# Second block's attention: where the pieces of the differential values' projection are computed, how that half's value products are cut, and when kept results are split

## The reference

```python
out_a: sc = qg . ka * scale;  p = softmax(sc);  o = p @ va           # 8 heads of 64, 2 key/value heads
# out_b, the differential half: 4 heads, each with two score maps and values of width 128
sc = jnp.einsum('bqhjd,blhjd->bhjql', q, kb).astype(jnp.float32) * scale
p = jax.nn.softmax(sc, axis=-1)
w = (p[:, :, 0] - lam * p[:, :, 1]).astype(vb.dtype)
o = jnp.einsum('bhql,blhe->bqhe', w, vb)
o = rms_norm(o, subln_g) * (1.0 - lam_init)
...
x = x + jnp.einsum('ble,ed->bld', jnp.concatenate([out_a, out_b], axis=-1), w_out[l])
```

## Time and profile before

| | us |
|---|---|
| median of 3 runs | 2335.97 (2335.66 to 2338.61) |
| the profiled execution | 2333.98 |
| its span in the trace | 2332.20 |
| PE busy | 2273.7 (97% of the span) |
| attention loop, from the scores of step 0 to those of step 31 | 1767.08 to 1905.10 |
| start of the output projection after it | 1920.22 |

### The profile page before, as it was taken

The page is one execution under the profiler, slowest core; times in us unless marked ns, Lnnn a source line. Parts: engine busy times, 40 slices in busy tenths (PEclk is TensorE's granted clock), DMA queues, the critical chain, the costliest instruction groups (busy, mean ns, idle before and its releaser), DMA issues.

```text
span 2332.2 us, 30970 instructions
## 1 busy us (share of the span) xinstructions
PE 2273.7 (97%) x11139; PEld 1841.0 (79%) x11139; DVE 1007.9 (43%) x1598; ACT 613.0 (26%) x1083; POOL 1459.9 (63%) x1452
## 2 busy tenths in 40 slices
PE   8999999999999999999999999999999889999999
PEld 7767887888888887678878888888977557888887
DVE  6975553532331049657535333211384453333200
ACT  4333324221110023343242211110244552111100
POOL 6644665876667756546648767667493236767663
PEclk9999999999999999999999999999999999999999
DMA  5321333322332233212334232232330102332232
GB/s 183 100 72 55 95 103 112 133 97 93 99 99 92 98 116 101 72 55 95 96 117 137 91 99 98 91 99 92 121 114 16 37 1 77 104 99 95 94 100 81
DMA packets 69861, 217.37 MB, mean 93 GB/s; under 512 B 8448, under 2 KB 10752, under 8 KB 69632
## 3 DMA queue, kind: packets, MB, share of 16 engines
q1 hardware_dynamic: 54016, 188.41, 25.2%
q10 hardware_dynamic: 15744, 27.52, 3.3%
HBM read 195.93 MB, written 10.49 MB: 89 GB/s over the span
## 4 chain that ended last, share of the span: by engine, by line
PE 90%; DVE 6%; ACT 2%; issue 1%; ACTq 0%; DMA 0%; POOL 0%; DVEq 0%; POOLq 0%
PE ps L1665 78%; PE ps L1985 2%; PE ps L2150 2%; DVE score L1449 1%; DVE small L1445 1%; PE ps L1931 1%; ACT pe L1013 1%; PE ps L1916 1%; PE ps L2210 1%; PE ps L2170 1%; PE ps L1944 1%; PE ps L2028 1%; PE ps L2212 1%; PE ps L2015 0%; PE ps L2079 0%
## 5 line engine op out<-in xcount | busy, mean ns | idle before, releaser
L536 POOL TENSOR_TENSOR w_lo<-w_raw,w_hi 128x512 fp32r<-128x512 f32 x700 | 951.4, 1359 | 58.4
L533 POOL TENSOR_SCALAR w_hi<-w_raw 128x512 fp32r<-128x512 f32 x700 | 487.0, 696 | 680.1 <-DMA w_raw<-wst 651.3
L1665 PE MATMUL ps<-h_hi,w_lo 128*128 128x512 f32 (+1 forms) x2056 | 803.8, 391 | 20.0 <-issue 4.9
L1665 PE MATMUL ps<-h_lo,w_hi 128*128 128x512 f32 (+1 forms) x2056 | 784.9, 382 | 0.0
L1665 PE MATMUL ps<-h_hi,w_hi 128*128 128x512 f32 (+1 forms) x2056 | 784.8, 382 | 0.0
L1665 PEld LDWEIGHTS ps<-h_hi,w_lo 128*128 128x128 f32 x2056 | 387.5, 188 | 121.0 <-issue 33.4
L1665 PEld LDWEIGHTS ps<-h_lo,w_hi 128*128 128x128 f32 x2056 | 387.9, 189 | 77.7 <-issue 6.2
L1665 PEld LDWEIGHTS ps<-h_hi,w_hi 128*128 128x128 f32 x2056 | 387.4, 188 | 75.4
L1665 PE MATMUL ps<-a_hi,w_lo 128*128 128x512 f32 (+1 forms) x572 | 213.7, 374 | 0.0
L1665 PE MATMUL ps<-a_hi,w_hi 128*128 128x512 f32 (+1 forms) x572 | 213.2, 373 | 0.0
L1665 PE MATMUL ps<-a_lo,w_hi 128*128 128x512 f32 (+1 forms) x572 | 213.2, 373 | 0.0
(11 more groups left out here) (301 smaller groups left out, 2570.5 us busy)
## 6 DMA issues: line engine op xcount, KB each, us to landing
w_raw<-wst SPq DMA_DIRECT2D x350, 512.0 KB, 3.5
rot<-raw ACTq DMA_DIRECT2D x70, 128.0 KB, 3.3
gates<-gt ACTq DMA_DIRECT2D x32, 256.0 KB, 4.2
stage<-gates ACTq DMA_DIRECT2D x32, 256.0 KB, 3.0
x_sb<-xin SPq DMA_DIRECT2D x8, 256.0 KB, 5.6
out<-x_sb SPq DMA_DIRECT2D x8, 256.0 KB, 4.5
kc<-cst ACTq DMA_DIRECT2D x1, 1056.0 KB, 4.9
kc<-cst SPq DMA_DIRECT2D x1, 417.0 KB, 8.0
```

Of the source, the lines that this page charges most:

```text
L533: eng.tensor_scalar(w_hi[s][:, part], w_raw[s][:, part], 1.0, 1.0, ALU.mult, ALU.mult)\
L536: eng.tensor_tensor(w_lo[s][:, part], w_raw[s][:, part], w_hi[s][:, part].bitcast(F32), ALU.subtract)\
L1665: m = eng.matmul(o, w, x, start=first and i == 0, stop=final and i == 2)
```

## The change

Three edits, all in this loop.

1. The filler's pieces are put elsewhere. Token block 1 is made in steps 0 to 3 (3, 3, 1 and 1 pieces), block 2 in steps 6 to 8, block 3 in steps 10 to 12, and the meta tokens in steps 14 to 16. Steps 0 to 4 held two token blocks before; step 4 now has no filler. The total is the same.
2. The products of units 4 to 7 are cut by token blocks: `values_differential(u, b)` issues four matmuls of 128 columns in the step with t-3 = 4u+b, ahead of that step's transposes, and waits only for the copy of block b. The meta part comes with b = 3. `values_before` gives the count on `v2_done` that the copies wait for. The loop on PE still ends with the same step.
3. The kept results' high halves are made in steps 19, 20 and 21 on ACT, their low halves in steps 20, 21 and 22 on DVE (before: 15, 16 and 17 on both). Since unit 3's result is now split first, the output projection takes k in the order 3, 0, 1, 2, 4, 5, 6, 7.

```diff
-VB_FILLS = {0: (1, range(0, 4)), 1: (1, range(4, 8)), 2: (2, range(0, 3)), 3: (2, range(3, 6)), 4: (2, range(6, 8)),
-            6: (3, range(0, 2)), 7: (3, range(2, 5)), 8: (3, range(5, 8)),
-            10: (4, range(0, 2)), 11: (4, range(2, 5)), 12: (4, range(5, 8))}
+VB_FILLS = {0: (1, range(0, 3)), 1: (1, range(3, 6)), 2: (1, range(6, 7)), 3: (1, range(7, 8)),
+            6: (2, range(0, 2)), 7: (2, range(2, 5)), 8: (2, range(5, 8)),
+            10: (3, range(0, 2)), 11: (3, range(2, 5)), 12: (3, range(5, 8)),
+            14: (4, range(0, 2)), 15: (4, range(2, 5)), 16: (4, range(5, 8))}
+KEPT_AT = TB * PAIRS_A + 3
+SPLIT_ORDER = [3, 0, 1, 2, 4, 5, 6, 7]
...
+def values_before(u, b):
+
+    return 2 * u + b // 2 + 1 if u < PAIRS_A else 2 * PAIRS_A + TB * (u - PAIRS_A) + b + 1
...
             def kept_split(u):
-                eng.wait_ge(w_used, index[(L2, "vb3")] + 1)
+                acc((L2, "vb3"))
                 eng.wait_ge(y2_kept, u + 1)
                 eng.activation(h_hi[:, u, :], kept[u][:, :], ACT.Copy).then_inc(ysp_hi, 1)
...
-                if 0 <= t - TB * PAIRS_A + 1 < KEPT:
-                    kept_split(t - TB * PAIRS_A + 1)
+                if 0 <= t - KEPT_AT < KEPT:
+                    kept_split(t - KEPT_AT)
...
-                if 0 <= t - TB * PAIRS_A + 1 < KEPT:
-                    result_lower(t - TB * PAIRS_A + 1)
+                if 0 <= t - KEPT_AT - 1 < KEPT:
+                    result_lower(t - KEPT_AT - 1)
...
+            def values_differential(u, b):
+
+                eng.wait_ge(t2_taken[b % 2], turns_before(u) + b // 2 + 1)
+                if b == 0 and u == PAIRS_A:
+                    eng.wait_ge(ysp_lo, 8 * L2 + 1)
+                    taken(eng, (L2, "vbm"))
+                elif b == 0:
+                    eng.wait_ge(y2_taken, u - PAIRS_A)
+                cols = slice((u - PAIRS_A) * P, (u - PAIRS_A + 1) * P)
+                toks = slice(b * P, (b + 1) * P)
+                y = bank(7)
+                for kb in range(TB):
+                    m = eng.matmul(y[:, toks], vb_sb[:, kb, cols], pt2[0][:, kb, toks], start=b + kb == 0, stop=False)
+                m.then_inc(v2_done, 1)
+                if b == TB - 1:
+                    eng.wait_ge(tm_taken, u + 1)
+                    eng.matmul(y, vbm_sb[0:META, cols], ptm[0:META, :], start=False, stop=True).then_inc(y2_ready, 1)
...
-                if b == 0 and u > 0:
+                if b == 0 and 0 < u <= PAIRS_A:
                     values(u - 1, 1)
-                if b == 2 and u >= 0 and u < UNITS:
+                if b == 2 and 0 <= u < PAIRS_A:
                     values(u, 0)
+                if t - LAG - 1 >= TB * PAIRS_A:
+                    values_differential(*divmod(t - LAG - 1, TB))
```

More of the change, by code:

```diff
@@ L2120, in values_in @@
                     begin((L2, f"vb{n}" if n < TB else "vbm"))
-                    if n > 2:
-                        eng.wait_ge(tm_taken, n - 2)
+                    if n > 1:
+                        eng.wait_ge(tm_taken, n - 1)
                 toks = slice(n * P, (n + 1) * P)
@@ L2189, in values @@
                 for i in range(2):
[L2190 removed]
+                    eng.wait_ge(t2_taken[i], turns_before(u) + 2 * j + 2)
                 if j:
@@ L2207, in values @@
                 for kb in range(TB):
[L2208 to L2212 removed]
+                    for i in range(2):
+                        m = eng.matmul(y[rows[i], toks], va_sb[:, kb, rows[i]], pt2[i][:, kb, toks], start=j + kb == 0, stop=False)
                 m.then_inc(v2_done, 1)
[L2214 to L2216 removed]
+                if j:
                     for i in range(2):
                         m = eng.matmul(y[rows[i]], vmz[0:2 * META, rows[i]], ptm[0:2 * META, :], start=False, stop=True)
[L2219 to L2221 removed]
+                    m.then_inc(y2_ready, 1)
+            def values_differential(u, b):
[14 more added lines that the diff above has]
+                    eng.matmul(y, vbm_sb[0:META, cols], ptm[0:META, :], start=False, stop=True).then_inc(y2_ready, 1)
             def o_square_2(h):
@@ L2247, in _ @@
             cs = [chunk((L2, f"wo{i}")) for i in range(4)]
-            for k in range(KT):
-                if k == 2:
+            for n, k in enumerate(SPLIT_ORDER):
+                if n == 2:
                     o_square_2(HH - 1)
-                eng.wait_ge(ysp_lo, 8 * L2 + k + 1)
+                eng.wait_ge(ysp_lo, 8 * L2 + n + 1)
                 for i in range(4):
-                    m = product(bank(i), *weights(cs[i], k), h_hi[:, k, :], h_lo[:, k, :], k == 0, k == KT - 1)
-                    if k == KT - 1:
+                    m = product(bank(i), *weights(cs[i], k), h_hi[:, k, :], h_lo[:, k, :], n == 0, n == KT - 1)
+                    if n == KT - 1:
                         m.then_inc(w_used, 1)
```

30 lines of the change are left out of this document (6 added, 24 removed).

## The result

The changed kernel took 2324.56 us (median of 7 runs, 2323.86 to 2331.0) against 2335.97 for the kernel before (7 runs, 2335.08 to 2340.38): ratio 0.995, 95% interval 0.9938 to 0.9962. In the later measurement the gain of the medians was 9.7, also more than the 7.1 forecast, but its interval, 4.9 to 11.9 us, holds the 7.1; that of the first measurement, 8.9 to 14.5, does not. The profiled execution took 2324.15 (span 2322.3, mean granted clock 0.997).

A forecast was written before the change was run, and what follows sets the result against it. PE was taken to bound the kernel, with a softmax floor of 3.56 us per attention step. Terms 4.0-3.0+2.4+3.1+0.6 = 7.1 us, off the median 2335.97, gave 2328.9 us, range 2326.8 to 2332.5.

The forecast's parts named there:

- Filler, steps 0 to 4: Attention loop, steps 0 to 4: with fewer filler pieces they fall from 22.36 to 18.32, a gain taken as 4.0.
- The floor of 3.56: Attention loop: the softmax loop lets no step take less than 3.56, whatever PE has less; read from step 5.
- The first rival: Steps 0 to 3 stay as long as before, no floor in unit 0: gain only 4.5, 2331.5 us; chance 5%.
- Filler, steps 14 to 16: Steps 14 to 16 take the meta pieces and the shape of steps 6 to 8: 13.93 becomes 16.95, a loss of 3.02.
- Kept results: Steps 17 and 18 without the two conversions: 10.67 becomes 8.26, a gain of 2.41.
- Differential products: Steps 19 to 30, a quarter of the unit per step at 0.96: 46.48 becomes 43.41, a gain of 3.07.
- The rival that a quarter costs as much as a half: Differential products: weight loads decide, so the whole gain falls to 1.8, 2334.2 us, no change; chance 4%.
- the lower clock in steps 19 to 30: Rival: PE's lower clock level is granted in steps 19 to 30, making the whole 20 slower, 2356 us; chance 3%.
- Behind step 31: Step 31 to output projection, before 15.12: 13.8 at full clock or 15.2 to 16.1 at half; gain taken as 0.6.
- The sum against the medians: The summed gain of 7.1 set against the median 2335.97, with some 1 us either way from the medians.
- C: Theory formed after the first runs: pauses the change removes sometimes let the clock fall, costing before some 0.7 on average.
- U in its other form: Theory from the experiments: some effect of the changed program other than its length moves time ahead of the loop.

The follow-up runs named there:

- kept_alone: The kernel before with only the kept results split in steps 19 to 22 and the new order of k: 2330.7 us, ratio 0.9988.
- cut_in_place: The kernel before with each half of the differential products issued as two quarters in the half's own step: 2335.5 us, ratio 0.9998.
- early_split: The changed kernel with wo2 to wo5 split inside the loop (steps 21 to 28) and step 31's transposes moved ahead: 2323.79 us, ratio 0.9943 to before.
- again: The changed kernel without an edit, measured again later: 2325.6 us, ratio 0.9964 to the kernel before.
- before_2: The kernel before without an edit, a second trace: step 16 took 6.91 in place of 5.28.
- before_3: The kernel before without an edit, a third trace: step 20 took 5.23 in place of 3.63.
- fill_alone: The kernel before with only the filler's new places: 2334.55 us, ratio 1.0003.
- diff_alone: The kernel before with only the differential products cut by token blocks: 2330.05 us, ratio 0.9979.
- tail_order: The changed kernel with only the last step's transposes put ahead of unit 7's first values: 14.04 us from step 31 to the output projection.
- before_busy: The kernel before with twenty needless matmuls added at the pauses of steps 16 to 20: 2337.56 us, ratio 1.0.

## Why the prediction was wrong in size and right in direction

**Filler, steps 0 to 4: right.** 3.99 against 4.0. The floor of 3.56 holds in unit 0 too; PE waits 0.58 for ACT in steps 3 and 4. The first rival falls.

**Filler, steps 14 to 16: right.** +3.01, the shape of steps 6 to 8.

**Kept results: right.** Steps 17 and 18 took 8.22 against 8.26. `kept_alone` gains 3.8, since there the wait of step 16 goes too, which in the whole change lies inside the 3.0 of the filler.

**Differential products: mechanism right, sizes off.** -2.27 against -3.07. A quarter costs 1.00 ahead of transposes and 1.09 ahead of the meta part (start to start), not the 0.96 I took, so a meta step is 3.91 and not 3.79 (three times 0.12). The sum of squares costs 0.95 and not the 0.5 I took from no row (the trace of before has the same two matmuls as a row of 1.02 at 1906.78); with 0.12 of waiting for ACT's copy of transposed weights ahead of the quarter, the steps that hold it are 3.70 (twice 0.14). Steps 20, 24 and 28 are 3.62, as one step of each unit was before (three times 0.06). Together this is the 0.8 that is missing. `cut_in_place` shows the cut by itself at 0.06 a half, so a quarter inside a run is (1.92+0.06)/2 = 0.99, which is what stands ahead of transposes; the 0.1 more ahead of the meta part I can only name. The estimate by the rule of the Trainium skill ("TensorE: Matmul & The Clock Gate", section "Back-to-back issue gap"), 1.4 a quarter, is farther off than the row's 0.89. The rival that a quarter costs as much as a half falls, as does the lower clock in steps 19 to 30: granted 1.00 there in all seven traces of kernels with the quarters in the loop.

**Behind step 31: right by luck.** -0.55 against -0.6. I had two cases, 13.8 at full clock and 15.2 to 16.1 at half clock, and took a value between them. Neither came: the clock fell again, but it was back at the upper level for the last quarter and the meta part (1.23 and 1.12), and the tail took 14.57. What I did not ask is what makes the tail long at all. It is POOL's splits behind the loop, by the wait for `wo3` and by DVE's slower operations beside them: without the splits it is 10.5 (`early_split`). The transposes' order and the clock are worth at most 0.8 while they stay.

**The sum against the medians: this step failed.** I took the sum of the stretch, put it under the median of the three runs of before and allowed "some 1 us either way from the medians". The sum was 0.8 too large, and yet the medians differed by 11.4, 5.1 more than the stretch. The term that was mis-sized is that 1 us. What stood in its place is the mean granted clock: it was 0.9967 in the first seven of the changed kernel, against 0.9947 in the 82 later runs of the kernel before, and 0.0020 at 2.1 us for 0.001 is 4.2 us. (The clock of the runs of the kernel before in the first measurement is on record for one alone, 0.996.) Runs of the same kernel spread over 15 us by it, since falls of the clock come in some executions and not in others, ahead of the loop too. At equal clock the two kernels are 6.7 apart with 0.9 either way, which is the stretch. Step 0, behind code that is the same in all, started between 1763.5 and 1772.0 in the traces. In the first pair of traces there was one more fall ahead of step 0 before than after, worth 1.7 of the 3.55; the other 1.8 is not in the clock, and no run says where it comes from. The fall lies in one window (140 to 148 us), in which the trace of before and then that of after read:

```profile
140.00:148.00 8.00, 5.56 (x23) 2.62 (x22) 6.42 (x18) 0.60 (x1) 6.33 (x7) 0.79 0.19 67
```

```profile
140.00:148.00 8.00, 6.62 (x34) 4.39 (x35) 5.28 (x19) 2.30 (x10) 5.06 (x6) 1.00 0.20 67
```

and `again` and `before_2` read 1.00 there, each with falls elsewhere. Why the mean clocks differ is only in part known. Supported but not settled is that the pauses of steps 16 to 20 which the change removes cost the kernel before 1.6 more in some executions (3 of 7 traces). I had read one trace, in which they did not, and put the clock there at 1.00 as if it were the kernel's.

**What stays open.** Over all runs the mean clock is 0.9947 before (82 runs) and 0.9961 for the changed kernel (19 runs with the first seven). The difference has a standard error of 0.0004, so scatter alone is an unlikely account of it, though the 12 runs of `again` by themselves are only 0.0008 above the 35 beside them, with an error of 0.0005. By 2.1 us for 0.001 it is 2.9 us. C would give 0.7 of it. A second part lies behind step 31. In three traces of kernels that still end with a half (`before_3`, `fill_alone`, `cut_in_place`) the clock stayed down for longer there than in the other four, and the time up to the end of the program was 1.7, 1.7 and 3.1 longer. In none of the four traces that have a quarter there and a fall (`after`, `again`, `diff_alone`, `tail_order`) did it. The same 9 us from the start of that half in `before` and in `before_3`:

```profile
1915.83:1924.83 9.00, 9.00 (x30) 6.61 (x31) 0.00 (x0) 1.24 (x2) 8.67 (x10) 0.84 0.01 3
```

```profile
1917.84:1926.84 9.00, 9.00 (x22) 5.73 (x23) 0.00 (x0) 1.23 (x2) 8.67 (x10) 0.62 0.01 3
```

Over seven traces that is 0.9 us on average, an estimate, as thin as C's. The rest would lie ahead of step 0, where the code is the same. Step 0 starts at 1767.6 on average in the eight traces of kernels without the whole change and at 1765.6 in the six with it, but single traces of the two overlap (1764.5 to 1772.0, 1763.5 to 1767.7). Whether that is chance or U in its other form, these runs don't tell. Nor do the parts: `kept_alone` and `before_busy`, with fewer or partly filled pauses, have a mean clock of 0.9952 and 0.9953, and `diff_alone`, with the pauses, 0.9959.

## What to carry to other kernels

Steps that are limited by a chain of two engines have a floor, and moving work from steps above it to steps at it gains the overhang, to a few hundredths; price each instruction group with its change-over to the next, not by the rate inside a group. Before a gain of half a per cent is set against medians, look how far the executions of the unchanged kernel spread and whether each follows its own granted clock; compare at equal clock, or compare the stretch, and remember that either leaves out what the change does to the clock. And where a stretch waits for work that could stand elsewhere and an engine takes twice its usual time beside that work, as behind step 31 for POOL's splits, ask for that first: moving the splits was worth 3.5 there, the reorder 0.5.

## What the runs showed of the hardware

- **DVE beside POOL.** In these traces only DVE operations with two inputs from SBUF slow down: the difference from 0.76 to as much as 1.86 (at 1866.59 in `early_split`), the low half from 0.69 to 1.76, the scaling from 0.75 to 1.75. Those that read PSUM don't: in `early_split` a copy and a maximum that lay wholly beside a subtraction of POOL took 0.68 and 0.70, as they do alone. POOL's subtraction too stretches from 1.27 to 1.76. It is the one that starts second that grows: the difference at 1870.50 in `early_split` took 0.76 and the subtraction behind it 1.71, the difference at 1874.20 took 1.45 and the subtraction already under way 1.27. The Trainium skill ("SBUF — State Buffer", section "Who interferes with whom") says that a DVE instruction with two SBUF inputs contends with a GpSimd instruction that reads SBUF. The rows agree in which operations are hit.
- **The clock behind short pauses.** Pauses of PE of 1.1 to 1.7 us, in steps in which it was otherwise busy, were followed by the lower level in some executions and not in others, with identical instructions (`before` against `before_2` and `before_3`). The pause in the tail (3.3 to 3.5 us, 1.73 in `tail_order` behind one of 0.50) was followed by it in every trace; where it was filled, or only 0.71 long, it was not.
- **Small fp32 products.** A quarter, four products of 128 columns: 1.16 as a group, 1.00 to 1.09 start to start, 0.06 more than half of a half inside one run.
